# Seven block products in place of eight for pairs of feed-forward steps, with two weight sums made by adding DMAs

## The reference

```python
def swiglu(x, w_in, w_out):
    gate, up = jnp.split(x @ w_in, 2, axis=-1)
    return (jax.nn.silu(gate) * up) @ w_out
# order: ffn, gla mixer, ffn | ffn, retention mixer, ffn | attention block with a relu-squared ffn
h = layer_norm(DN_ALPHA * h + 0.5 * swiglu(h, ffn_w_in[i, 0], ffn_w_out[i, 0]), ln_g[i, 0], ln_b[i, 0])
```

## Time and profile before

| | |
|---|---|
| runs | 1515.93 us median (1515.62, 1515.93, 1516.52) |
| profiled execution, first to last instruction | 1514.4 us |
| profiled execution's own time | the page gives no other than its span |
| PE / DVE / ACT / POOL busy | 1506.3 / 977.3 / 765.7 / 126.8 us |
| bytes moved | 284.75 MB, mean 188 GB/s |

### The profile page before, as it was taken

The page is one execution under the profiler, slowest core; times in us unless marked ns, Lnnn a source line. Parts: engine busy times, 40 slices in busy tenths (PEclk is TensorE's granted clock), DMA queues, the critical chain, the costliest instruction groups (busy, mean ns, idle before and its releaser), DMA issues.

```text
span 1514.4 us, 20467 instructions
## 1 busy us (share of the span) xinstructions
PE 1506.3 (99%) x8086; PEld 1293.6 (85%) x8086; DVE 977.3 (65%) x1043; ACT 765.7 (51%) x775; POOL 126.8 (8%) x128
## 2 busy tenths in 40 slices
PE   9999999999999999999999999999999999999998
PEld 8888888888888888888888888888998888888886
DVE  6555677765557555577567755557687556775565
ACT  6454466544545454454434445445536566354443
POOL 0100020200002000023021200002002200020000
PEclk9999999999999999999999999999999999999999
DMA  7655554465454545464545554556444434455551
GB/s 283 246 201 200 188 221 167 149 240 195 166 204 192 216 167 201 187 246 172 192 149 172 194 216 169 200 189 245 149 167 143 164 139 167 167 216 201 187 185 71
DMA packets 43128, 284.75 MB, mean 188 GB/s; under 512 B 5185, under 2 KB 5633, under 8 KB 10417
## 3 DMA queue, kind: packets, MB, share of 16 engines
q1 hardware_dynamic: 38592, 270.35, 48.8%
q0 software_dynamic: 2656, 9.64, 1.9%
q10 hardware_dynamic: 1808, 3.74, 0.6%
HBM read 282.60 MB, written 1.05 MB: 187 GB/s over the span
## 4 chain that ended last, share of the span: by engine, by line
PE 99%; DMA 0%; ACT 0%; issue 0%; DVE 0%; POOLq 0%; POOL 0%; DVEq 0%
PE psum L1799 21%; PE psum L1693 16%; PE psum L1696 16%; PE psum L1697 16%; PE psum L1803 11%; PE psum L1826 6%; PE psum L1833 3%; PE psum L1725 2%; PE psum L1738 2%; PE psum L1731 2%; PE psum L1705 1%; PE psum L1957 1%; PE psum L2223 0%; PE psum L2186 0%; PE psum L2244 0%; PE psum L2077 0%
## 5 line engine op out<-in xcount | busy, mean ns | idle before, releaser
L969 DVE TENSOR_TENSOR weights_lo<-weights_raw,weights_hi 128x2048 fp32r<-128x2048 f32 x247 | 566.4, 2304 | 318.5 <-ACT weights_hi L467 317.1
L467 ACT ACTIVATE weights_hi<-weights_raw 128x2048 fp32r<-128x2048 f32 (+1 forms) x254 | 479.5, 1889 | 301.9 <-PE psum L1697 142.2
L1799 PE MATMUL psum<-operand,weights_hi 128*128 128x512 f32 x1376 | 327.6, 390 | 0.0
L1799 PEld LDWEIGHTS psum<-operand,weights_hi 128*128 128x128 f32 x1376 | 255.3, 188 | 51.1
L1693 PE MATMUL psum<-weights_hi,hidden_hi 128*128 128x512 f32 x480 | 187.7, 391 | 0.0
L1696 PE MATMUL psum<-weights_lo,hidden_hi 128*128 128x512 f32 x480 | 187.6, 391 | 0.0
L1697 PE MATMUL psum<-weights_hi,hidden_lo 128*128 128x512 f32 x480 | 186.8, 389 | 0.0
L1803 PEld LDWEIGHTS psum<-operand,weights_lo 128*128 128x128 f32 x1376 | 176.4, 191 | 6.7
L1803 PE MATMUL psum<-operand,weights_lo 128*128 128x256 f32 x1376 | 178.5, 283 | 0.0
L1693 PE MATMUL psum<-weights_hi,operand 128*128 128x512 f32 x384 | 151.5, 394 | 0.0
L1696 PE MATMUL psum<-weights_lo,operand 128*128 128x512 f32 x384 | 149.8, 390 | 0.0
(11 more groups left out here) (312 smaller groups left out, 1782.5 us busy)
## 6 DMA issues: line engine op xcount, KB each, us to landing
weights_raw<-in_weights SPq DMA_DIRECT2D x254, 1024.0 KB, 4.8
ln_rows<-in_ln_rows POOLq DMA_DIRECT2D x16, 512.0 KB, 6.6
weights_raw<-in_weights SPq DMA_DIRECT2D x4, 256.0 KB, 4.5
weights_raw<-in_weights SPq DMA_DIRECT2D x2, 512.0 KB, 6.6
normalised<-in_x POOLq DMA_DIRECT2D x2, 512.0 KB, 7.4
ret_constants<-in_ret_constants ACTq DMA_DIRECT2D x1, 1024.0 KB, 7.4
out<-normalised SPq DMA_DIRECT2D x4, 256.0 KB, 2.0
normalised<-in_x_turned SPq DMA_DIRECT2D x3, 256.0 KB, 5.3
```

Of the source, the lines that this page charges most:

```text
L467: nc.scalar.activation(w_hi[:, s, whole], raw[:, s, whole], ACT.Copy).then_inc(hi_split, 1)
L969: nc.vector.tensor_tensor(w_lo[:, s, :], raw[:, s, :], w_hi[:, s, :].bitcast(F32), ALU.subtract).then_inc(lo_split, 1)
L1799: mm(banks[b // 2][:, b % 2, :], w_hi[:, slot, cols], x_both[:, c, :, :].rearrange("p a t -> p (a t)"), start=c == 0, stop=False, skip_gro ...
```

## The change

In each of the four layers steps 2 and 3, 5 and 6, 8 and 9 become a group. With x cut into four blocks (tokens x feature halves: x11, x12, x21, x22) and the weights of the pair into b11, b21 (first step, two row halves) and b12, b22 (second step), the two steps' gate and up are computed with seven products of 128 x 512 by 512 x 512 in place of eight, with sums of blocks of x (four "forms", once a layer) and of weights: t1 = b12 + b11 and t4 = b21 + t2 by DMAs issued on POOL that add into the destination, t2 = t1 + b22 and t3 = t2 - b11 on DVE, each in place of a raw tile. A sum's tile is split as any other, so a group has 9 operand tiles for its 6 loads and a layer 42 operands for 33 loads. ACT copies a bank out before the next product adds to it; DVE combines. The result has tokens on the partitions and is transposed as the first unit's is (`turn_group`, 8 transposes). There are up to 7 raw slots and 4 operand slots inside these layers; the added ones lie over the mixers' buffers, so in the second and fourth such layer their loads wait for the mixer's last tile. Slots come from tables. ACT's, DVE's, PE's and SP's loops are written out everywhere. `features_both` does its blocks bank pair by bank pair.

```diff
+GROUPS = (2, 5, 8)
+FORMS = ("b11", "t1", "b21", "t2", "b22", "t3", "down", "t4", "down")
+RAW_SLOTS, OPERAND_SLOTS = 7, 4
...
@@ SP
-                    sp.wait_ge(lo_split, i * RING + (n - RING + 1))
-                    sp.dma_start(raw[:, n % RING, :], src).then_inc(weight_loaded[n % RING], 16)
+            for m in range(RING, len(RAW_SLOT)):
+                if WIDE_LOAD[m] in (N_FFN1, N_FFN3) and WIDE_LOAD[m - 1] is None:
+                    sp.wait_ge(weights_used, WIDE_LOAD[m])
+                if RAW_AFTER[m]:
+                    sp.wait_ge(lo_split, RAW_AFTER[m])
+                sp.dma_start(raw_in(m), io["weights"][m]).then_inc(weight_loaded[RAW_SLOT[m]], 16)
@@ POOL: layer_norm, after the residual and before load_rows, calls add_t1 for the first group
+            def add_t1(n0, f, s):
+                n = n0 + GROUP_AT[s]
+                for load in (n, n + 1):
+                    pool.wait_ge(weight_loaded[RAW_SLOT[LOAD_OF[load]]], RAW_COUNT[LOAD_OF[load]])
+                pool.dma_start(raw_of(n + 1), raw_of(n), accum_op=ALU.add).then_inc(t1_added, 16)
+            def add_t4(n0, f, s):
+                n = n0 + GROUP_AT[s]
+                pool.wait_ge(lo_split, n + 3)
+                pool.wait_ge(tile_added, 2 * group_index(f, s) + 1)
+                pool.dma_start(raw_of(n + 7), raw_of(n + 3), accum_op=ALU.add).then_inc(t4_added, 16)
@@ ACT
+                split_hi(n0 + 3)
+                if f:
+                    keep_x((None, 2, 3, 5)[f])
+                split_hi(n0 + 4)
+                silu(n0, pairs[0][:, :, 0:TOK])
+                forms_hi()
+                second_of_next(2, n0 + 5)        # split_hi of t1, waits for t1_added
+                act.wait_ge(hid_turned, f + 1)
+                hidden_hi(j0, 0, two(acc[:, 3, :]))
+                summed_step(1, n0 + 4, 2)
...
+                    split_hi(n + 3, (tile_added, 2 * g + 1))
+                    copy_back(n + 1, p1, 0)
+                    split_hi(n + 4)
+                    copy_back(n + 2, p5[:, :], 1)
+                    split_hi(n + 5, (tile_added, 2 * g + 2))
+                    copy_back(n + 4, p6, 0)
+                    split_hi(n + 6)
+                    split_hi(n + 7, (t4_added, 16 * g + 16))
...
@@ DVE
+                split_lo(n0 + 3)
+                form_sums()
+                hidden(j0, pairs[0][:, :, TOK:2 * TOK])
+                split_lo(n0 + 4)
+                forms_lo()
+                split_lo(n0 + 5)
+                hidden_lo(j0, 0, two(acc[:, 3, :]))
+                summed_step(1, 2)                # two sums, add_t2, hidden, split_lo of b21, hidden_lo
...
+                    split_lo(n + 3)
+                    add_t3()
+                    split_lo(n + 4)
+                    split_lo(n + 5)
+                    split_lo(n + 6)
+                    first_block()
+                    less(p6, 1, n + 5, 3)
+                    less(p5[:, :], 0, n + 6, 2)
+                    split_lo(n + 7)
...
@@ PE
+                def product(n, b, x, start):
+                    w_hi_n, w_lo_n = hi_of(n), lo_of(n)
+                    parts = [(x(0, k), x(1, k), slice(k * NCOL, (k + 1) * NCOL)) for k in range(4)]
+                    pe.wait_ge(hi_split, n + 1)
+                    for k, (a_hi, a_lo, cols) in enumerate(parts):
+                        mm(work[:, b, :], a_hi, w_hi_n[:, cols], start=start and k == 0, stop=False, skip_group_check=True)
+                        mm(work[:, b, :], a_lo, w_hi_n[:, cols], start=False, stop=False, skip_group_check=True)
+                    pe.wait_ge(lo_split, n + 1)
+                    for k, (a_hi, a_lo, cols) in enumerate(parts):
+                        last = mm(work[:, b, :], a_hi, w_lo_n[:, cols], start=False, stop=k == 3, skip_group_check=True)
+                    last.then_inc(weights_used, 1)
+                def group(s, n, pairs_free):
+                    g = group_index(f, s)
+                    product(n, 0, block_of_x(0, 0), True)
+                    product(n + 1, 1, form(0), True)
+                    pairs_free()
+                    product(n + 2, 2, block_of_x(0, 1), True)
+                    pe.wait_ge(copied_back, 3 * g + 1)
+                    product(n + 3, 0, form(1), False)
+                    pe.wait_ge(copied_back, 3 * g + 2)
+                    product(n + 4, 1, form(2), False)
+                    pe.wait_ge(copied_back, 3 * g + 3)
+                    product(n + 5, 0, form(3), False)
+                    next_down(s - 2, n + 6)
+                    pe.wait_ge(combined, 3 * g + 3)
+                    product(n + 7, 0, block_of_x(1, 1), False)
+                    next_down(s - 1, n + 8, {(1, 0, 1): lambda: turn_group(g, s)})
```

More of the change, by code:

```diff
@@ L59, with ffn_units, ffn_loads @@
 N_TILES = N_FF2 + 4 * FF2_STEPS
+FFN_STARTS = (N_FFN0, N_FFN1, N_FFN2, N_FFN3)
 LAYER_STARTS = (N_FFN0, N_GLA, N_FFN1, N_FFN2, N_RET, N_FFN3, N_SEC, N_FF2, N_TILES)
+def ffn_units():
+    units, s = [], 2
+    while s < FFN_STEPS:
+        units.append(s)
+        s += 2 if s in GROUPS else 1
+    return units
+def ffn_loads():
+    loads = [("up", s, half) for s in range(2) for half in range(2)]
+    for s in ffn_units():
+        if s in GROUPS:
+            loads += [("up", s, 0), ("up", s + 1, 0), ("up", s, 1), ("up", s + 1, 1), ("down", s - 2), ("down", s - 1)]
+        else:
+            loads += [("up", s, 0), ("up", s, 1), ("down", s - 2)]
+    return loads + [("down", FFN_STEPS - 2), ("down", FFN_STEPS - 1)]
@@ new lines, with ffn_operands @@
+FORMS = ("b11", "t1", "b21", "t2", "b22", "t3", "down", "t4", "down")
+def ffn_operands():
+    operands = [(load, 1) for load in ffn_loads()[:4]]
+    for s in ffn_units():
+        if s in GROUPS:
+            b11, b12, b21, b22 = ("up", s, 0), ("up", s + 1, 0), ("up", s, 1), ("up", s + 1, 1)
+            operands += [(b11, 0), (b12, 0), (b21, 0), (b12, 0), (b22, 1), (b11, 1), (("down", s - 2), 1), (b21, 1), (("down", s - 1), 1)]
+        else:
+            operands += [(("up", s, 0), 1), (("up", s, 1), 1), (("down", s - 2), 1)]
+    return operands + [(("down", FFN_STEPS - 2), 1), (("down", FFN_STEPS - 1), 1)]
@@ L551, in summed_step @@
                     nc.scalar.activation(silu_g[:, :, :], gate_up[:, 0:2, :], ACT.Silu).then_inc(silu_done, 1)
[L552 to L561, removed]
+                    if after in GROUPS:
+                        split_hi(n0 + GROUP_AT[after] + 2)
@@ L1129, in ffn @@
[L1129 to L1134 removed]
+                    if after in GROUPS:
+                        add_t2(after)
+                    dve.wait_ge(hid_ready, j0 + j)
+                    dve.wait_ge(up_summed, summed_before(f, j) + 1)
+                    hidden(j0 + j, gate_up[:, 2:4, :])
@@ new lines, in group_hidden_lo @@
+                def group_hidden_lo(s):
+                    for k in range(2):
+                        hidden_lo(j0 + s + k, (s + k) % 3, two(work[:, 2 + k, :]))
+                split_lo(n0 + 3)
[6 more added lines that the diff above has]
+                summed_step(1, 2)
+                units = ffn_units()
@@ L2424, in ffn @@
               for s in range(FFN_STEPS)]
-        tiles = up[0] + up[1]
-        for s in range(2, FFN_STEPS):
-            tiles += up[s] + [down[s - 2]]
-        return tiles + down[-2:]
+        return [up[load[1]][load[2]] if load[0] == "up" else down[load[1]] for load in FFN_LOADS]
     tiles = ffn(0, 0)
```

528 lines of the change are left out of this document (359 added, 169 removed).

## The result

The changed kernel takes 1523.64 us (1523.35 to 1525.36), the kernel before, run beside it, 1515.99: a ratio of 1.0052, 95% interval 1.0040 to 1.0065, 7.65 us slower. The forecast was 1517 us, +0.9 us in the span; the span grew by 7.1 us, from 1514.4 to 1521.5. The forecast itself was a change within 0.2%, and that is not what came: 1523.64 lies at the upper edge of its own range (1511 to 1524). The chances given were 0.40 for faster by over 0.2%, 0.19 for within and 0.41 for slower, so the direction was left open.

What follows compares the result with a forecast made beforehand. PE was taken as the bound, busy 1506.3 of 1514.4 us. Saving -28.7 and first-group stalls +29.6 gave +0.9, span 1515.3; with the runs' median 1.5 above the span, 1516.8, called 1517 us, own range 1511 to 1524.

Steps and rivals of the forecast that it cites:

- The saving: PE in every pair of steps: seven products plus transposes save 2.39 us a pair, 28.7 us in all.
- Middle groups without a stall: Eight mid-layer groups: DVE's splits are ready in time, tightest at the first down by 0.45 us; stall 0, up to 1.
- Rival (c): Middle groups: DVE slips, the first down stalls 1 to 1.5 us, 8 to 12 in all: 1527 us; chance 0.07.
- The slack of t1 in these groups: Groups after a layer's first: t1 is issued some 10 us before ACT wants it; PE stalls only from 18 us.
- The first group's stall, max(2.7, X - 4.8): PE at the first down of each layer's first group: 14.5, 5.6, 3.9 and 5.6 us, 29.6 in all.
- X: Landing of the first t1 add, from the second unit's start: 19.3, 10.4, 8.7 and 10.4 us by layer.
- the lower bound: Each layer's first group: DVE's own queue makes the first down late by 2.7 us, however early the add lands.
- The size of the add: Adding DMA, issue to landing: 11 us (8 plus 2.87 for reading the destination), 12 in layers two and four, 13.5 in the first.
- The frame at zero: Written-out loops, block order in a unit and changed waits elsewhere: no PE instruction added, cost taken as zero.
- that late hidden: First layer: a late tile 4 delays the first hidden by 2 us, inside the 14.5 us stall there.
- the sign that I named for the saving: PE's total busy time should fall by some 29 us; if not, the saving itself is wrong.

Runs made afterwards that it cites:

- e4: The changed kernel with t1 left unsummed in each layer's first group (b12 used as loaded): 1502.25 us, ratio 0.9908.
- e8: As e4, with DVE's sum of t2 in the first groups also cut to one column: 1501.42 us, ratio 0.9904.
- e5: The changed kernel with all 24 adding DMAs made plain copies of the same size: 1513.09 us, ratio 0.9983.
- e6: The changed kernel with SP issuing each feed-forward layer's seventh load only after the first t1 has been added: 1514.27 us, ratio 0.9988.
- e1: The changed kernel without any groups or adding DMAs, only the rest of the change kept: 1517.93 us, ratio 1.0017.
- e2: The changed kernel with groups at steps 5 and 8 only, steps 2 and 3 left plain: 1500.98 us, ratio 0.9903.

## Why the prediction was right, and where it was off

- **The saving** (2.39 us a pair, 28.7 in all): 2.30 and 27.6. The seven products came to 19.04 us (19.11 predicted), the transposes to 0.79 (0.72), the two down products took the rest.
- **Middle groups without a stall**, by a walk through DVE's queue with 0.45 us to spare: right in seven of eight, 0.3 us short in the first layer's group at step 5. DVE's 2.20 us a tile, 0.045 less than the walk had, is in its favour. Rival (c) is out. The slack of t1 in these groups was smaller than stated, though. The prediction had PE stall only from a landing of 18 us; the group that was 0.3 us late had its t1 land after 13.0, and ACT had waited 6.80 us for it. (The nine splits are the right number, but they are four sums, b11, b21, b22 and two down tiles.)
- **The first group's stall, max(2.7, X - 4.8)**: the mechanism held. The first down product started at X + 22.8 in three layers (X + 23.6 in the first, where a split beside POOL's residual took 3.13 us) against X + 23.15; the lower bound measured 2.56 in e4, but in e8 only 0.8 of it went with 2.2 us less work on DVE, so its size came out better than its reason. Stalls of 14.5, 5.6, 3.9 and 5.6 were predicted; by layer lengths (length - 149.72 + 6.90) they were 14.8, 7.3, 3.5 and 7.9.
- **The size of the add** is the term that was off: 11 us alone, 12 in the second and fourth layer. It is 6.9 alone and 13.6 and 14.4 there. The two errors nearly cancelled because all four adds that matter fall in a crowd; the third layer's 10.8 matched 11 for the wrong reason. I had priced a plain copy at 8 us and the crowd at 1 to 2.5. e5 and e6 show a quiet copy at 4.6, the sum at 2.3 more (2.87 predicted) and the crowd at 3.9 to 7.5. In the second layer X was 12.3 instead of 10.4; stalls of 29.6 us were forecast and 33.5 came, the second and fourth layer giving all of the excess.
- **The frame at zero**: e1 shows 1.2 us, nearly all of it in the first layer's first unit. In the changed kernel that late hidden is 2 us and lies inside the first layer's 14.8, as the prediction had it; only 0.1 us at the start and the 1.1 us after the last store's issue stand outside the layers.
- **Clock**: not in the sum. A stall counted to the moment when the down tile is ready already holds the slow matmuls inside it, so they cost nothing on top. But the sign that I named for the saving, PE's busy time falling by 29 us, fails (16.3) for a saving that is there; e2, with hardly a gap, shows 18.7 for eight pairs.

The sum is then -27.6 + 33.5 + 1.2 = +7.1 us, where -28.7 + 29.6 + 0 = +0.9 was forecast. Of the 6.2 us between, 3.9 are the stalls, 1.1 the saving, 1.2 the start and the end. That the total came so near is in part luck: two wrong sizes cancelled in the add. Not settled: why the fourth layer's add took 14.4 us and the second's 13.6 with the same loads around them, and by what mechanism the end grows with POOL's tile DMAs.

## What to carry to other kernels

Less work on the engine that is the bound pays only where the helpers' queue has slack at that place: the same pair of steps gave 2.3 us in mid-layer and cost 5.7 at a layer's opening, so make the change per place, and time it per place. Work moved into DMAs should be priced beside the loads that are pending when it is issued, and the wait for it put down with everything behind it on the waiting engine. When a wait on a start-up path is removed, look for the next in the same queue before counting the gain.

## What the runs showed of the hardware

- An SBUF-to-SBUF DMA of 1 MB from POOL's queue takes 4.6 us as a copy and 6.9 as an add when it is alone (engines' share 0.58 and 0.74); with loads pending (share 0.96 to 1.0) 7.9 to 11.0 and 10.8 to 14.4. The issuing instruction holds POOL for 0.53 us as a copy, 0.84 as an add. After the last store's issue the program ended 0.6 us later with 16 such DMAs than with none, 0.9 with 20 and 1.2 with 24.
- POOL's arithmetic and DVE slow each other: one residual with DVE idle took 1.05 us (kernel before, at 72.19), two beside one DVE split 4.13, and two beside the first group's unbroken DVE work 12.04 in the first layer; the last DVE split next to them took 3.13 us in place of 2.29.
- PE ran at half clock for about 3.4 us after 2.7 us idle in a stretch of 7.2. In the first layer, after the transposes' wait of 1.85 us, 16 matmuls took 5.50 us in place of 3.90; after the same wait in e2, 1.90 us, they took 3.90 at full clock. So one length of wait was followed by either level.
